# Gate projection of a hybrid decoder layer as seven block products, with a new order of gating, stores and loads

## The reference

```python
h = h + f.astype(h.dtype)                       # f: the down projection of the FFN
gate = jax.nn.sigmoid(rmsnorm(h, norm_ple_w[i]) @ w_pg[i])
h = h + ((p[i] @ w_ple[i]) * gate).astype(h.dtype)
return rmsnorm(h, final_norm_w)
```

## Time and profile before

| | |
|---|---|
| time, median of 3 runs | 2188.81 us (2188.57 to 2189.2) |
| profiled execution, its own time | 2188.78 us |
| its span, first to last instruction | 2187.1 us |
| TensorE busy | 2168.5 us, 99% |
| VectorE, ScalarE, GpSimd busy | 1380.7, 885.3, 304.9 us |
| mean granted TensorE clock | 0.998 of full speed |

### The profile page before, as it was taken

One profiled execution on the slowest core, in us unless ns is written; L12 is line 12 of the kernel. 1 busy time (PEld: TensorE's weight loads), 2 busy tenths in 40 slices (PEclk: granted clock), 3 DMA queues, 4 the chain that ended last, 5 costly groups with the idle time before them and its releaser, 6 DMA issues.

```text
span 2187.1 us, 28802 instructions
## 1 busy us (share of the span) xinstructions
PE 2168.5 (99%) x10794; PEld 1834.3 (84%) x10794; DVE 1380.7 (63%) x1726; ACT 885.3 (40%) x1026; POOL 304.9 (14%) x329
## 2 busy tenths in 40 slices
PE   9999999999999999999999999999999999999997
PEld 7888878888888888888888888888888888888886
DVE  7486336453378988888888888886333333446444
ACT  6222246442243544445554454444222122226444
POOL 6993004000000111111111111110000000000001
PEclk9999999999999999999999999999999999999999
DMA  6422222134332877777777777766343332233222
GB/s 222 135 75 94 104 97 82 58 121 168 120 118 104 214 209 212 206 197 189 209 210 204 205 189 201 212 198 246 99 142 107 122 128 93 92 115 114 96 96 77
DMA packets 106181, 321.53 MB, mean 147 GB/s; under 512 B 8240, under 2 KB 57264, under 8 KB 85904
## 3 DMA queue, kind: packets, MB, share of 16 engines
q1 hardware_dynamic: 76400, 268.39, 34.3%
q0 software_dynamic: 29728, 52.44, 13.1%
HBM read 298.77 MB, written 22.02 MB: 147 GB/s over the span
## 4 chain that ended last, share of the span: by engine, by line
PE 89%; POOL 7%; ACT 1%; DVE 1%; DMA 1%; issue 0%; SPq 0%; POOLq 0%; DVEq 0%; ACTq 0%
PE bank L1016 23%; PE bank L686 17%; PE bank L687 17%; PE bank L688 17%; PE bank L1018 12%; PE bank L800 1%; DMA Y<-in_x 1%; ACT xs_hi L1126 0%; POOL QKV L2312 0%; POOL QKV L2332 0%; POOL Q L2353 0%; POOL Y L2348 0%; POOL Q L2358 0%; PE bank L870 0%; POOL QKV L2327 0%
## 5 line engine op out<-in xcount | busy, mean ns | idle before, releaser
L1016 PE MATMUL bank<-x_block,w_hi 128*128 128x512 f32 x2240 | 777.4, 391 | 1.2 <-DVE w_lo L1961 1.2
L1018 PE MATMUL bank<-x_block,w_lo 128*128 128x256 f32 x2240 | 629.0, 281 | 0.0
L1102 ACT ACTIVATE w_hi<-w_raw 128x2048 fp32r<-128x2048 f32 (+1 forms) x134 | 222.4, 1660 | 733.6 <-PE bank L688 720.9
L1016 PEld LDWEIGHTS bank<-x_block,w_hi 128*128 128x128 f32 x2240 | 419.6, 187 | 92.6 <-DVE w_lo L1961 1.5
L1018 PEld LDWEIGHTS bank<-x_block,w_lo 128*128 128x128 f32 x2240 | 423.3, 189 | 0.0
L686 PE MATMUL bank<-xs_hi,w_hi 128*128 128x512 f32 x1024 | 404.8, 395 | 2.7 <-DVE xs_lo L1578 2.2
L688 PE MATMUL bank<-xs_hi,w_lo 128*128 128x512 f32 x1024 | 398.8, 389 | 0.0
L687 PE MATMUL bank<-xs_lo,w_hi 128*128 128x512 f32 x1024 | 398.7, 389 | 0.0
L1554 DVE TENSOR_TENSOR w_lo<-w_raw,w_hi 128x2048 fp32r<-128x2048 f32 (+1 forms) x136 | 271.6, 1997 | 134.0 <-ACT w_hi L1102 131.4
L1403 ACT ACTIVATE w_hi<-Y 128x1024 fp32r<-128x1024 f32 x159 | 168.7, 1062 | 180.0 <-PE bank L1018 125.2
L686 PEld LDWEIGHTS bank<-xs_hi,w_hi 128*128 128x128 f32 x1024 | 192.2, 188 | 46.9 <-issue 5.6
(11 more groups left out here) (356 smaller groups left out, 2505.5 us busy)
## 6 DMA issues: line engine op xcount, KB each, us to landing
w_raw<-in_w_up SPq DMA_DIRECT2D x48, 1024.0 KB, 5.1
w_raw<-in_w_down SPq DMA_DIRECT2D x64, 704.0 KB, 4.1
Y<-in_w_up SPq DMA_DIRECT2D x40, 1024.0 KB, 6.0
w_raw<-in_w_in SPq DMA_DIRECT2D x31, 1024.0 KB, 4.9
Y<-in_w_up POOLq DMA_DIRECT2D x59, 512.0 KB, 6.8
Y<-in_w_up SPq DMA_DIRECT2D x39, 512.0 KB, 7.6
w_raw<-in_w_out SPq DMA_DIRECT2D x16, 1024.0 KB, 5.3
w_raw<-in_w_pg SPq DMA_DIRECT2D x16, 1024.0 KB, 4.7
```

Source lines behind the costliest of these rows:

```text
L1016: nc.tensor.matmul(place(c, b, 0, 2), w_h[:, ks], xb[b][:, k, :, :].rearrange("p e t -> p (e t)"), start=fresh and k == 0, stop=False, ski ...
L1018: last = nc.tensor.matmul(place(c, b), w_l[:, ks], xb[b][:, k, 0, :], start=False, stop=k == HALF_K - 1, skip_group_check=True)
L1102: nc.scalar.activation(w_hi[c % 2][:, 0:width], w_raw[c % 2][:, 0:width], ACT.Copy).then_inc(hi_made, 1)
```

## The change

The gate projection takes the scheme of the up-projection, for eight pairs of tiles (`gate_pair`), with three matmuls of 256 columns per k.

- Activations: `scale_h` multiplies h by the gain in place, after the unscaled row was stored to `h_dram` (`park_h`). The tiles of the last quarter come in the order of `last_row` (0, 8, 1, 9, ...), so that the blocks `gb` of the early products (A11, S1, S3, S2) are made row by row during that quarter (`first_sums`, `first_rests`, `second_rest` on VectorE, their high parts on ScalarE) and those of A12, A22, S4 in one piece each afterwards (`late_half`, `late_rest`). `xs_hi` and `xs_lo` of h are no longer made.
- PLE: over seven banks, copied by ScalarE to six slots and stored to `ple_dram`; each row is loaded again, one at a time, into one buffer (`ple_in_use`).
- rstd: sums per token with one-column matmuls after the first eight PLE tiles, Newton on [128, 4], a spread after the fourth product of pair 0.
- Weights: 512 KB blocks (`gate_raw_in`), four sums a pair on VectorE (`gate_s3`, `gate_s2`, `gate_s1`, `gate_s4`), seven high parts and seven rests of 1024 columns (`gate_half`, `gate_rest`) into the ring of four blocks.
- Results: VectorE puts the four quadrants together (`gate_m1`, `gate_u`, `gate_c22`, `gate_c11`, `gate_c21`, `gate_c12`) and multiplies with rstd; A12 waits for `u2`, A22 for `u3`, S4 for `c22`. ScalarE does sigmoids and squares. GpSimd now multiplies with the PLE row, adds to the reloaded h row and adds the squares for pairs 0 to 6 (`finish_row`, `add_squares`, six operations a pair); VectorE does it for the last pair.
- SyncE: parks and PLE stores are issued ahead of later loads, as in the excerpt. Rows 14 and 15 change places at the end.

The diff, cut to its core:

```diff
+OUT_ORDER = [6, 7, 8, 0, 9, 10, 1, 11, 12, 2, 13, 15, 3, 14, 4]
+PLE_SLOTS = 6
+PLE_BANKS = [3, 4, 5, 6, 7, 0, 1] * 2 + [3, 0]
...
+def last_row(j):
+    return j // 2 + HALF_K * (j % 2)
...
+        def gate_raw(c, b):
+            upper, lower = w_raw[0], w_raw[1]
+            s4_place = Y[:, KT - 2:KT, :].rearrange("p k t -> p (k t)") if c < GATES - 1 else lower[:, 0:BLOCK]
+            return {A11: upper[:, 0:BLOCK], S1: upper[:, 0:BLOCK], A12: upper[:, BLOCK:], S4: s4_place,
+                    S3: lower[:, 0:BLOCK], S2: lower[:, 0:BLOCK], A22: lower[:, BLOCK:]}[b]
...
+            def park_h(i):
+                sp.wait_ge(h_kept, 16 * (KT + 2 * i))
+                for s in range(2):
+                    sp.wait_ge(evacuated, DOWN_END - KT + 2 * i + s + 1)
+                    j = last_row(2 * i + s)
+                    sp.dma_start(h_dram[:, j, :], Y[:, j, :]).then_inc(h_kept, 16)
...
+                    if q == QUARTERS - 1 and i == 0:
+                        sp.wait_ge(mid_out, 16 * FT)
+                        sp.wait_ge(mid_lo_made, FT)
+                        sp.dma_start(p_raw[:], A["p"]).then_inc(p_landed, 16)
...
-                    weights(PG0 + s, i, A["w_pg"][2 * i + s], W_FULL)
+            park_h(KT // 2 - 2)
+            park_h(KT // 2 - 1)
...
+            for b in (S3, A22):
+                gate_raw_in(0, b)
+            for j in range(KT):
+                if j == 3:
+                    for b in (A11, A12):
+                        gate_raw_in(0, b)
+                sp.wait_ge(ple_out, j + 1)
+                sp.dma_start(ple_dram[:, j, :], ple_stage[:, j % PLE_SLOTS, :]).then_inc(ple_sent[j % PLE_SLOTS][0], 16)
+            ple_all_sent(sp)
+            sp.wait_ge(sq_used, 3 * KT)
...
+            for c in range(GATES):
+                if c:
+                    ple_row_in(2 * c - 1)
+                if c < GATES - 1:
+                    gate_raw_in(c + 1, S3)
+                    gate_raw_in(c + 1, A11)
+                    gate_raw_in(c + 1, A12)
+                    gate_raw_in(c + 1, A22)
+                if c:
+                    ple_row_in(2 * c)
+                    h_rows_in(c)
+            sp.wait_ge(blk_lo, gate_index(GATES - 1, S1) + 1)
...
+                    if PLE_BANKS[j] in PLE_BANKS[:j]:
+                        pe.wait_ge(ple_out, j - PLE_BANKS[:j][::-1].index(PLE_BANKS[j]))
+                    elif PLE_BANKS[j] < 2:
+                        pe.wait_ge(evacuated, DOWN_END)
...
-            spread_sum(3 * KT, ss[:], bank[2])
-            with pe.Fori(0, KT // 2) as i:
-                for s in range(2):
...
+            def gate_pair(c):
+                for b in range(PRODUCTS):
+                    pe.wait_ge(blk_lo, gate_index(c, b) + 1)
+                    if c == 0:
+                        pe.wait_ge(gb_lo, GB_LO + 4 * HALF_K + (LATE.index(b) + 1 if b in LATE else 0))
+                        if b == 0:
+                            pe.wait_ge(ple_out, KT - 2)
+                    if c == 1 and b == 0:
+                        pe.wait_ge(evacuated, DOWN_END)
+                        pe.wait_ge(ple_out, KT)
+                        pe.wait_ge(rstd_made, 3)
+                    if c >= 2 and b == 0:
+                        pe.wait_ge(c12_made, FAST + c - 1)
+                    if b == A12:
+                        pe.wait_ge(u2_made, FAST + c + 1)
+                    if b == A22:
+                        pe.wait_ge(u3_made, FAST + c + 1)
+                    if b == S4:
+                        pe.wait_ge(c22_made, FAST + c + 1)
+                    fresh = b in (S3, S2, A11, S1)
+                    w_h, w_l = ring(w_hi, FAST + c, b), ring(w_lo, FAST + c, b)
+                    for k in range(HALF_K):
+                        ks = slice(k * P, (k + 1) * P)
+                        last = product(place(FAST + c, b), w_h[:, ks], w_l[:, ks], gb[b][:, k, 0, :], gb[b][:, k, 1, :],
+                                       fresh and k == 0, k == HALF_K - 1, onto=True)
+                    last.then_inc(product_done, 1)
+                    if c == 0 and b == S1:
+                        spread(diag_made, 3, c_value, bank[2], rstd_spread)
+            for c in range(GATES):
+                gate_pair(c)
...
+            pe.wait_ge(ss_added, SS_ADDED + KT - 2)
+            pe.wait_ge(value_sq, VALUE_SQ + GATES)
+            for e, src in enumerate((h_ss[:], c_value)):
+                for j in range(4):
+                    nc.tensor.matmul(sums[:, j:j + 1], src[:, j * P:(j + 1) * P], ones[:, 0:1],
+                                     start=e == 0 and j == 0, stop=False, skip_group_check=True)
...
+            def ple_copy(j):
+                if j >= PLE_SLOTS:
+                    ple_row_sent(act, j - PLE_SLOTS)
+                act.wait_ge(ple_done, j + 1)
+                nc.scalar.activation(ple_stage[:, j % PLE_SLOTS, :], bank[PLE_BANKS[j]][:], ACT.Copy).then_inc(ple_out, 1)
...
+            ple_copy(2)
+            first_sums_half(7)
+            for j in range(3, 6):
+                ple_copy(j)
+            second_sum_half(7)
+            for j in range(6, 8):
+                ple_copy(j)
+            late_half(A12, B21)
+            for j in range(8, 10):
+                ple_copy(j)
+            gate_half(0, A11)
+            ple_copy(10)
+            gate_half(0, S3)
+            for j in range(11, KT):
+                ple_copy(j)
+            gate_half(0, S2)
+            gate_half(0, S1)
+            late_half(A22, T4)
+            root(2, norm4[:, 1, :], norm4[:, 0, :])
+            late_half(S4, B22)
...
+            for c in range(GATES):
+                if c:
+                    gate_half(c, S1)
+                    gate_sigmoid(c, c_gate, gate_ready, gate_made)
+                gate_half(c, A12)
+                if c:
+                    gate_square(c, c_value, 2 * c - 1, value_h, value_sq)
+                gate_half(c, A22)
+                gate_half(c, S4)
+                if c:
+                    gate_square(c, c_gate, 2 * c - 2, h_made, gate_sq)
+                if c == 0:
+                    act.wait_ge(rstd_spread, 3)
+                    nc.scalar.activation(rstd[:], bank[2][:], ACT.Copy).then_inc(rstd_made, 1)
+                if c < GATES - 1:
+                    gate_half(c + 1, A11)
+                    gate_half(c + 1, S3)
+                    gate_half(c + 1, S2)
+                    gate_sigmoid(c + 1, c_value, value_ready, value_sig)
+                    if c >= 1:
+                        scale_pair(c - 1)
+                else:
+                    scale_pair(c - 1)
+                    gate_sigmoid(GATES, c_gate, gate_ready, gate_made, in_half(0))
+                    gate_sigmoid(c + 1, c_value, value_ready, value_sig)
+            gate_square(GATES, c_gate, KT - 2, h_made, gate_sq, in_half(0))
+            gate_square(GATES, c_value, KT - 1, value_h, value_sq)
+            gate_sigmoid(GATES + 1, c_gate, gate_ready, gate_made, in_half(1))
+            act.wait_ge(value_sq, VALUE_SQ + GATES)
+            scale_out(KT - 1)
...
+            first_rests(6)
+            second_rest(6)
+            first_sums(7)
+            w_rest(PLE0 + 1)
+            first_rests(7)
+            second_rest(7)
...
+            def gate_u(c):
+                dve.wait_ge(product_done, gate_index(c, S2) + 1)
+                sp2 = place(FAST + c, S2)
+                tt(gu2, sp2, gu2, ALU.subtract).then_inc(u2_made, 1)
+                dve.wait_ge(u2_made, FAST + c + 1)
+                tt(gu3, gu2, place(FAST + c, S3), ALU.subtract).then_inc(u3_made, 1)
...
+                dve.wait_ge(last_ple, LAST_PLE + 16)
+                link(tt(part, part, w_raw[0][:, in_half(e)], ALU.mult))
+                dve.wait_ge(h_back, H_BACK + 16 * GATES)
+                tt(y, y, part, ALU.add).then_inc(h_made, 1)
+            late_rest(A12, B21)
+            gate_s3(0)
+            gate_rest(0, A11)
+            gate_rest(0, S3)
+            gate_s2(0)
+            gate_s1(0)
+            gate_rest(0, S2)
+            gate_rest(0, S1)
+            late_rest(A22, T4)
+            dve.wait_ge(ple_done, KT)
+            dve.wait_ge(sum_spread, 3)
+            rms_small(bank[2], 1.0 / D, var_made, root_made, diag_made, 3, c_value)
+            gate_rest(0, A12)
...
+            for c in range(GATES):
+                if c:
+                    gate_c12(c - 1)
+                    gate_rest(c, S1)
+                    gate_m1(c)
+                    gate_rest(c, A12)
+                else:
+                    gate_m1(c)
+                gate_rest(c, A22)
+                gate_u(c)
+                gate_rest(c, S4)
+                gate_c22(c)
+                if c < GATES - 1:
+                    gate_s3(c + 1)
+                    gate_rest(c + 1, A11)
+                if c == 0:
+                    dve.wait_ge(rstd_made, 3)
+                gate_c11(c)
+                if c < GATES - 1:
+                    gate_rest(c + 1, S3)
```

(29 more changed lines are left out.)

402 lines of the change are left out of this document (276 added, 126 removed).

## The result

| | before | after |
|---|---|---|
| time, median of 5 runs | 2188.81 us (2188.55 to 2189.2) | 2201.06 us (2198.02 to 2201.63) |
| ratio, 95% interval | | 1.0053 (1.0038 to 1.0067) |
| profiled execution, its own time | 2188.78 us | 2201.21 us |
| its span | 2187.1 us | 2199.7 us |
| mean granted TensorE clock | 0.998 | 0.995 |

The change makes the kernel 12.3 us slower by the medians (0.56%; 0.53% by the ratio); the forecast was 2188.2, the range ended at 2200.

The account below looks back on a forecast made before the run. TensorE's matmul stream, busy 99% of the span, was taken as the bound. From 2188.8 us, -12.2 + 0.8 + 6.1 + 2.7 + 2.0 = -0.6 gave 2188.2 us; range 2181 to 2200, the forecast's own 2185 to 2193.

Parts of the forecast that it names:

- block products: Gate stage on TensorE: 1344 matmuls of 256 columns at 0.1204 us, 161.8 us against 174.0; -12.2 us.
- small matmuls: Gate stage: one f32 spread goes, eight one-column matmuls and one spread come, in line; +0.8 us.
- opening: Start of the gate stage: TensorE waits before PLE tiles 8 and 15 and before A12 of pair 0; +6.1 us.
- rival 3: The clock: TensorE's 4.3 us stand before A12 of pair 0 can lower it; +3.0, 2191.2 us; chance 0.07.
- turns: Steady pairs: VectorE and GpSimd instructions with two SBUF operands alternate, u2 0.35 us late each pair; +2.7 us.
- tail: Last product to first output multiplication: later square of row 15, sixteen one-column matmuls, ten warm-ups; +2.0 us, 9.2 in all.
- the DMAs free: Gate stage loads: 3.1 MB a pair in 20.2 us, blocks needed 6 us and more later; cost nothing.
- Rival 2: Turns decide, slower: GpSimd operations of 1.5 us give 2197, 1.6 give 2202 us; chance 0.25.

Follow-up runs that it names:

- e1: Changed kernel with GpSimd's operations of pairs 0 to 6 on 32 of 512 columns, leaving out part of the computation; 2189.8 us.
- e10: Changed kernel with GpSimd's six operations a pair moved to VectorE and u2 ahead of the rest of A22 in pairs 1 to 7; 2193.6 us.
- e2: Changed kernel with GpSimd's operations of pairs 0 to 6 on 256 of 512 columns, leaving out part of the computation; 2189.4 us.
- e5: Changed kernel with VectorE making u2 and u3 before the rest of A22 in every pair; 2195.7 us.
- e6: Changed kernel with the h row added by a GpSimd-issued DMA, so GpSimd computes four operations a pair instead of six; 2201.7 us.
- e3: Changed kernel with 18 warm-up matmuls after pair 0's spread and 6 after the last product; 2197.9 us.
- e7: Changed kernel with m1 and u2 earlier in pair 0's VectorE order and earlier requests for pair 1's weight blocks; 2197.7 us.
- e9: Changed kernel with the weight sum S3 of pairs 2 to 7 made by a GpSimd-issued adding DMA instead of VectorE; 2213.6 us.
- e12: e10 with m1 and u2 earlier in pair 0's VectorE order and earlier requests for pair 1's weight blocks; 2189.9 us.
- e15: e10 with m1 and u2 earlier in pair 0's VectorE order, without early loads; 2193.8 us.
- e13: e12 with a new tail: h's sums right behind the last product, three warm-ups before row 15's sums, four instead of ten after; 2185.5 us.
- e14: e13 with the copy of A11's product (m1) made by ScalarE instead of VectorE in pairs 1 to 7; 2183.1 us.
- e8: Changed kernel with e6's addition by DMA, e5's order, e7's pair 0 order and early loads, and the tail edit of e13; 2199.1 us.
- e4: Changed kernel with pair 0's VectorE order alone: m1 and u2 before the last activation rest and S4's sum; 2200.5 us.

## Why the prediction was wrong

Measured terms are from the two profiled executions (after less before, 12.4 us).

| term | predicted | measured |
|---|---|---|
| block products, 56 x 2.88 against 174.0 | -12.2 | -12.7 |
| small matmuls | +0.8 | +0.8, not told apart |
| opening: w_lo 0.74, PLE copy 1.04, wait before A12 4.35 | +6.1 | +6.1 |
| opening: half clock in A12 | 0 (rival 3: 3.0) | +1.6 |
| turns, pairs 1 to 7 | +2.7 | +10.7 |
| tail (7.4 before, 12.8 after) | +2.0 | +5.4, of it 3.2 half clock |
| rest (not told apart) | 0 | +0.5 |

- **The rate of the products was right.** Starts 0.120 us apart, a product 2.88, the price of the weight loads hidden.
- **The opening was right to 0.1 us**, 4.35 for 4.3 before A12; 0.74 for 1.1 before PLE tile 8 and 1.04 for 0.7 before tile 15 miss by 0.35 each and cancel, which is luck. What it was worth was not foreseen: removing the 4.4 us alone gained nothing, because the blocks of pair 1 arrive late. The prediction had called the DMAs free ("their need is 6 us and more later"); VectorE stood 3.88 us for them, hidden behind the other wait. In the changed kernel that cost nothing (e1, e10: pair 1 in 20.2 us with the same late blocks); it is a second limit that shows once the first is gone.
- **The step that failed is the size of the turns.** The mechanism was named, with its engines and the instruction (`u2` behind the rest of A22), but `u2` came so late that TensorE stood 1.15 us, not 0.35, and the pair was 21.54 and not about 20.6 us; pair 1, 22.7 us, lost 2.5 where 0.56 was forecast. I added up only the instructions with two SBUF operands (13.6 + 7.7) and gave 21.3 as the upper bound. An engine works in order: whatever stands behind a blocked instruction stands too, the ones that read PSUM as well. The sum to make is VectorE's whole list, 17.1 us, and the time it is held. The schedule left room for 3.5 us held in its 20.6; the runs show 4.0 (busy times of e1 and the changed kernel) to 4.5 (21.54 less 17.1, so no measurement of its own). The edits to the amount of GpSimd's work (e1, e2), to the engine that does it (e10) and to the order alone (e5) leave no other cause for the length of the pairs.
- **The rival that came true, came for another reason.** Rival 2 gave the time (2197 to 2202) with GpSimd operations of 1.45 to 1.6 us. The operations recorded at 1.55 to 2.3 us contain their own waiting; by themselves they take 1.28 to 1.30 (additions of squares in e6 that began with no such instruction of VectorE under way), as the forecast assumed. So "the longer ones contain the blocking" was right, and no argument against the rival. That the time fell into the rival's span is luck besides: with the turns as measured and no half clock the forecast's sum would give 2196.2.
- **The clock.** Rival 3 came true in pair 0, at 1.6 and not 3.0 us; alone it was worth 0.1, as e3 shows. In the tail the forecast put the clock at nothing without a reason: 1.31 us without work were followed by 6 us at 1.2 GHz. With the clock held (e3, 9.6 us) the tail costs 2.2, close to the 2.0 predicted; the half clock is the other 3.2.
- **Sum.** The misses are 8.0 us for the turns, 4.8 for the clock (1.6 in pair 0, 3.2 in the tail) and 0.2 for the rest of the tail; -0.5 for the products and +0.5 not told apart cancel. That is 13.0 between the profiled executions, 12.9 by the median.

Not settled: why the clock fell in some executions of a kernel and not in others, and how the 0.5 us not told apart divide.

## What to carry to other kernels

Before giving elementwise work to an idle GpSimd, add to VectorE's whole list the time it will be held, not only compare the operations that share operands; here six operations cost VectorE 0.67 to 0.75 us each on GpSimd and 0.61 on VectorE itself. A wait in front of the bounding engine is worth only what the next wait behind it leaves, so look at what each engine stood for while the first wait covered it. A short idle time of TensorE ahead of a long row of tiny matmuls is cheap to fill, and can cost two times: the wait, and the half clock behind it. And a total in which the clock varies by 5 us does not tell two kernels 2 us apart; compare the stretch that the edit concerns.

## What the runs showed of the hardware

- VectorE and GpSimd with two SBUF operands each end in strict turn: one 1024-column VectorE and one 512-column GpSimd instruction together take 2.2 us, and each record shows the other's time in its own (1.22 becomes 2.31, 1.3 becomes 2.09 to 2.27). Each of the three GpSimd records shown ends some 1.15 us after the VectorE instruction in whose time it began.
- 1.31 us without a matmul in the tail was followed by the fall to 1.2 GHz in most executions and not in all: of the eleven kernels that have this gap the profiled execution shows the fall in eight and the clock at 1.00 in three (e5, e7, e9); the mean clock was 0.994 to 0.998 in the runs of e1, e2, e10, e12 and e15, and 0.997 or 0.998 in all 22 runs of e3, e13 and e14, in which the gap is filled. In e8 a gap of 0.85 us was followed by the fall. The Trainium skill (TensorE: Matmul & The Clock Gate, Part 1) says of a kernel's start that the number of matmuls at the low clock differs between runs of one kernel; no run here counts those, but the tails differ in the same way.
- The length of a wait alone does not decide what the clock does behind it. Behind 4.35 us in pair 0 (changed kernel, e1, e2, e10), 2.7 in e4, 2.42 in e6 and 1.74 in e7 a product ran at half clock (4.4 to 4.5 us in place of 2.88); behind 3.21 us in e5, 2.02 in pair 7 of e6 and 1.77 in pair 1 of the changed kernel it ran at full clock (2.93 to 2.95).
- A DMA that adds onto SBUF, issued by GpSimd among the weight loads of the gate stage, lands 6.4 us (256 KB, e6) or 9.0 us (512 KB, e9) after its issue by the median; plain loads of 512 KB in the same runs take 5.6 and 5.3 us, 4.6 in the changed kernel. Its issue takes 0.88 us of GpSimd.
